# Cache tiles kept with rows innermost, turned through two banks, with the second set of compression weights loaded by halves

## What is computed

```python
def compress_blocks(x, pe, w1, w2):
    B, Tk, H, D = x.shape
    r = CMP_BLOCK // CMP_STRIDE
    c = x.reshape(B, Tk // CMP_STRIDE, CMP_STRIDE, H, D)
    n_cmp = Tk // CMP_STRIDE - r + 1
    blocks = jnp.concatenate([c[:, j:j + n_cmp] for j in range(r)], axis=2)
    blocks = blocks + pe[None, None, :, None, :].astype(x.dtype)
    flat = jnp.moveaxis(blocks, 3, 2).reshape(B, n_cmp, H, CMP_BLOCK * D)
    return jax.nn.silu(flat @ w1) @ w2
...
k_cmp = compress_blocks(kv[:, :, 0], cmp_pe[0], cmp_w1[0], cmp_w2[0])
v_cmp = compress_blocks(kv[:, :, 1], cmp_pe[1], cmp_w1[1], cmp_w2[1])
```

## Time and profile before

| | us |
|---|---|
| median of three runs | 1488.47 (1487.07 to 1491.72) |
| the profiled execution | 1491.82 |
| its span, first to last instruction | 1490.2 |
| PE / DVE / ACT / POOL busy | 1316.0 / 818.9 / 341.5 / 195.6 |
| PE idle before turns, by DVE's copies to `kT` (L1724) | 34.6 |
| products: PE busy at L829, 1024 instructions | 167.6 |
| sums: DVE busy at L1739, 64 instructions | 109.1 |

### The profile page before, as it was taken

One profiled execution on the slowest core, in us unless ns is written; L12 is line 12 of the kernel. 1 busy time (PEld: TensorE's weight loads), 2 busy tenths in 40 slices (PEclk: granted clock), 3 DMA queues, 4 the chain that ended last, 5 costly groups with the idle time before them and its releaser, 6 DMA issues.

```text
span 1490.2 us, 26361 instructions
## 1 busy us (share of the span) xinstructions
PE 1316.0 (88%) x10160; PEld 1060.0 (71%) x10160; DVE 818.9 (55%) x1658; ACT 341.5 (23%) x895; POOL 195.6 (13%) x295
## 2 busy tenths in 40 slices
PE   7996898748884889899999999987788879999996
PEld 3453676537774678789999975675555458999996
DVE  1805546656665666166677429517623405677752
ACT  2114434323320222110000011236734311000000
POOL 0102000101201110111111011060012211111100
PEclk9996799859997999999999999857889989999998
DMA  7438597856636354145444543260036664454340
GB/s 251 155 114 291 193 344 257 290 160 200 196 113 227 115 193 146 33 138 163 131 142 134 195 154 129 63 176 1 1 120 193 197 212 134 149 170 152 118 156 33
DMA packets 148704, 236.14 MB, mean 158 GB/s; under 512 B 10562, under 2 KB 111170, under 8 KB 148162
## 3 DMA queue, kind: packets, MB, share of 16 engines
q1 hardware_dynamic: 140370, 204.00, 41.5%
q0 software_dynamic: 8208, 30.44, 6.2%
HBM read 229.09 MB, written 13.64 MB: 163 GB/s over the span
## 4 chain that ended last, share of the span: by engine, by line
PE 74%; DVE 12%; issue 4%; DMA 3%; SPq 3%; ACT 3%; POOL 0%; POOLq 0%; DVEq 0%; ACTq 0%
PE ps L745 18%; PE ps L540 10%; PE ps L770 10%; PE ps L504 10%; PE ps L829 4%; PE ps L713 4%; DVE big L1739 4%; PE ps L645 2%; PE ps L723 2%; PE ps L843 2%; PE ps L950 2%; PE ps L546 1%; SPq L390 1%; SPq L496 1%; DMA ring<-in_state_win 1%
## 5 line engine op out<-in xcount | busy, mean ns | idle before, releaser
L504 PE MATMUL ps<-ct,ring 128*128 128x128 f32 x960 | 149.9, 296 | 58.3 <-DVE kT L1724 34.6
L504 PEld LDWEIGHTS ps<-ct,ring 128*128 128x128 f32 x960 | 111.7, 149 | 104.0 <-issue 61.7
L829 PE MATMUL ps<-big,proj 128*128 128x168 f32 (+1 forms) x1024 | 167.6, 318 | 17.9 <-DMA proj<-in_cmp_w 15.5
L829 PEld LDWEIGHTS ps<-big,proj 128*128 128x128 f32 x1024 | 155.7, 198 | 24.0 <-DMA proj<-in_cmp_w 15.7
L540 PE MATMUL ps<-ring,xT 128*128 128x512 f32 (+1 forms) x384 | 161.3, 576 | 2.7 <-DMA ring<-in_w_in 2.7
L540 PEld LDWEIGHTS ps<-ring,xT 128*128 128x128 f32 x384 | 70.1, 193 | 81.5 <-issue 78.3
L745 PE MATMUL ps<-kT,proj 128*128 128x144 f32 x960 | 124.2, 286 | 0.0
L745 PEld LDWEIGHTS ps<-kT,proj 128*128 128x128 f32 x960 | 120.3, 190 | 0.0
L1078 ACT ACTIVATE big<-ps 128x512 f32<-128x512 f32 (+3 forms) x172 | 87.1, 532 | 112.4 <-PE ps L504 112.2
L2010 POOL DMA_DIRECT2D ring<-in_cache_kv x64 | 35.2, 550 | 382.1 <-issue 225.9
L1981 POOL TENSOR_TENSOR big<-rows 128x576 f32<-128x576 f32 x22 | 51.0, 2317 | 261.4 <-DVE rows L1638 228.1
(11 more groups left out here) (293 smaller groups left out, 2159.4 us busy)
## 6 DMA issues: line engine op xcount, KB each, us to landing
ring<-in_cache_kv SPq DMA_DIRECT2D x128, 512.0 KB, 5.8
ring<-in_w_gu SPq DMA_DIRECT2D x44, 1024.0 KB, 7.7
ring<-in_w_in SPq DMA_DIRECT2D x11, 2048.0 KB, 8.0
ring<-in_w_down SPq DMA_DIRECT2D x16, 1408.0 KB, 6.6
ring<-in_cache_kv SPq DMA_DIRECT2D x128, 128.0 KB, 3.0
ring<-in_cache_kv POOLq DMA_DIRECT2D x128, 128.0 KB, 3.2
ring<-in_w_out SPq DMA_DIRECT2D x4, 2048.0 KB, 9.1
ring<-in_state_win SPq DMA_DIRECT2D x16, 512.0 KB, 5.5
```

Of the source, the lines that this page charges most:

```text
L504: return nc.tensor.transpose(out, in_, C("ident", 0, rows, rows))
L829: last = mm(cmp_out(u, si, n), w1s(s, o)[:, hf * P:(hf + 1) * P], XS[(4 * kp + si) % XB][:, o, 0:n], start=o == 0, stop=o == 7)
```

## The change

1. `KR` is kept with rows innermost: a copy writes 8 x 32 elements, and the sums read every third element.
2. Turns go by two banks, 6 and 4 in turn, so each waits for the copies of the turn two back. `turn_o` of layer 0 moves from bank 4 to bank 7, with waits against `second` and `turn_weights0`, which use it too.
3. In the first round the turns and sums for tile 1 come one product later. DVE's `combine` moves from the last product of a unit to the first of the next, `silu_cmp` one further product on.
4. The value weights are loaded by halves of their columns: half 0 when 28 products are done, half 1 when 32 are; `sum_w1` goes by halves too, on DVE behind products 28 and 32.
5. Since `plan` follows `steps`, ring entries change places: tile 1 comes behind the fourth value load, not before it, and tile 2's slot is freed by the last turn of tile 1, no longer by a value step.
6. At the start the page table goes behind layer 0's first weights, SP does not wait for it, inputs are turned by column halves, and DVE scales the first half when three copies are done.

```diff
-        KR = [x.rearrange("p (h n o) -> p h n o", h=NKV, o=8)
+        KR = [x.rearrange("p (h o n) -> p h o n", h=NKV, o=8)
...
         for i in range(64):
             kp, a = i // 8, i % 8
-            if kp < 7 and a < 4:
-                steps.append(("turned", kp + 1, 2 * a))
+            ta = a - (kp == 0)
+            if kp < 7 and 0 <= ta < 4:
+                steps.append(("turned", kp + 1, 2 * ta))
...
-            if len(freed_at) >= SLOTS and freed_at[-SLOTS] > at[("product", 29, 1)] and (("w1r", 1), None, 0) not in plan:
-                plan.append((("w1r", 1), None, 0))
+            for hf in range(2):
+                if len(freed_at) >= SLOTS and freed_at[-SLOTS] >= at[("product", 26 + 4 * hf, 1)] and (("w1r", 1, hf), None, 0) not in plan:
+                    plan.append((("w1r", 1, hf), None, 0))
...
-            sp.wait_ge(s_page, 16)
...
                     else:
-                        sp.wait_ge(c_h, 30)
+                        cols = slice(name[2] * P, (name[2] + 1) * P)
+                        sp.wait_ge(c_h, 28 + 4 * name[2])
                     for t in range(2):
...
-                turn(ps[4][0:64, P:2 * P], osm[:, i % 2, :]).then_inc(v_t[l], 1)
+                if l == 0:
+                    pe.wait_ge(c_we, seconds_before[i])
+                turn(ps[7 - 3 * l][0:64, P:2 * P], osm[:, i % 2, :]).then_inc(v_t[l], 1)
...
-                if 8 * kp + g >= 1:
-                    pe.wait_ge(k_a[1], 8 * kp + g)
-                    pe.wait_ge(k_d[1], 8 * kp + g)
+                if 8 * kp + g == 1:
+                    pe.wait_ge(r_ps[0], 6)
+                    pe.wait_ge(r_sg, 6)
+                if 8 * kp + g >= 2:
+                    pe.wait_ge(k_a[1], 8 * kp + g - 1)
+                    pe.wait_ge(k_d[1], 8 * kp + g - 1)
                 for r in range(4):
                     a = (b2 * NPG + half * 4 + r) * KVW + i2 * P
-                    last = turn(ps[6][:, r * P:(r + 1) * P], cmp_src[0][:, a:a + P])
+                    last = turn(ps[6 - 2 * half][:, r * P:(r + 1) * P], cmp_src[0][:, a:a + P])
...
-                    if si == 0 and u >= 1:
+                    if si == 1 and u >= 1:
                         silu_cmp(u - 1)
...
-                x = ps[6][64:128, :].rearrange("p (n o r) -> p n o r", o=8, r=2)
+                x = ps[6 - 2 * half][64:128, :].rearrange("p (n o r) -> p n o r", o=8, r=2)
                 for par in range(2):
-                    last = v.tensor_copy(KR[b2][par * 64:par * 64 + 64, 2 * i2 + 1, 32 * half:32 * half + 32, :], x[:, :, :, par])
+                    last = v.tensor_copy(KR[b2][par * 64:par * 64 + 64, 2 * i2 + 1, :, 32 * half:32 * half + 32],
+                                         x[:, :, :, par].rearrange("p n o -> p o n"))
...
-                    x = [KR[b2][:, :, c:c + 3 * NG - 2:3, :].rearrange("p h m o -> p o h m") for c in range(4)]
+                    x = [KR[b2][:, :, :, c:c + 3 * NG - 2:3] for c in range(4)]
...
-                    if a % 4 == 3:
-                        combine(i // 4)
-                    if i == 31:
-                        sum_w1(1)
-                    if kp < 7 and 3 <= a < 7:
-                        sum_chunks(kp + 1, a - 3)
+                    if i == 63:
+                        combine(15)
+                    elif i and a % 4 == 0:
+                        combine(i // 4 - 1)
+                    if i in (28, 32):
+                        sum_w1(1, i // 32)
+                    sa = a - 3 - (kp == 0)
+                    if kp < 7 and 0 <= sa < 4:
+                        sum_chunks(kp + 1, sa)
```

More of the change, by code:

```diff
@@ L191, in rep @@
             return a.broadcast_to(shape)
-        s_page, s_x, s_first, s_const, s_kv, s_out, s_w1 = (sem(n) for n in ("s_page", "s_x", "s_first", "s_const", "s_kv", "s_out", "s_w1"))
+        s_gain, s_x, s_const, s_kv, s_out, s_w1 = (sem(n) for n in ("s_gain", "s_x", "s_const", "s_kv", "s_out", "s_w1"))
         s_slot = [sem(f"s_slot{i}") for i in range(SLOTS)]
@@ L294, in trunk @@
             steps.append(("product", i, 0))
-            if kp < 7 and a < 4:
-                steps.append(("turned", kp + 1, 2 * a + 1))
+            if kp < 7 and 0 <= ta < 4:
+                steps.append(("turned", kp + 1, 2 * ta + 1))
             steps.append(("product", i, 1))
@@ L304, in trunk @@
         at = {s: n for n, s in enumerate(steps)}
+        seconds_before = [sum(at[("second", k)] < at[("back", i)] for k in range(8)) for i in range(4)]
+        backs_before = [sum(at[("back", i)] < at[("second", k)] for i in range(4)) for k in range(8)]
         freed_at = []
@@ L420, in _ @@
             sp.dma_start(proj[0:TS, 2, 0:D], x_sample.rearrange("b q d -> (b q) d")).then_inc(s_x, 16)
-            sp.dma_start(gc[:], gcol).then_inc(s_first, 16)
-            sp.dma_start(pages[:], page_table.rearrange("b n -> (b n)").unsqueeze(0)).then_inc(s_page, 16)
+            sp.dma_start(gc[:], gcol).then_inc(s_gain, 16)
             def late_constants():
+                sp.dma_start(pages[:], page_table.rearrange("b n -> (b n)").unsqueeze(0)).then_inc(s_const, 16)
                 sp.dma_start(ct[:, n_first:], consts[:, n_first:]).then_inc(s_const, 16)
@@ L438, in _ @@
                     if name[1] == 0:
+                        cols = slice(0, CH)
                         sp.wait_ge(t_p[0], 12)
@@ L504, in turn @@
                 return nc.tensor.transpose(out, in_, C("ident", 0, rows, rows))
-            pe.wait_ge(s_x, 48)
-            pe.wait_ge(s_first, 32)
-            for t in range(3):
-                for j in range(2):
+            pe.wait_ge(s_x, 64)
+            for j in range(2):
+                for t in range(3):
                     for i in range(4):
@@ L777, in second @@
                     pe.wait_ge(c_we, kp)
+                if backs_before[kp]:
+                    pe.wait_ge(v_e[0], backs_before[kp])
                 for b2 in range(2):
@@ L1078, in copy @@
                 return f(out, in_, ACT.Copy)
-            for t in range(3):
-                for j in range(2):
-                    act.wait_ge(x_t, 2 * t + j + 1)
+            for j in range(2):
+                for t in range(3):
+                    act.wait_ge(x_t, 3 * j + t + 1)
                     v = ps[2 * t + j][:, :].rearrange("p (i n) -> p i n", i=4)
@@ L1246, in keep_cmp @@
                     act.wait_ge(c_x, 4 * kp)
-                x = ps[6][0:64, :].rearrange("p (n o r) -> p n o r", o=8, r=2)
+                x = ps[6 - 2 * half][0:64, :].rearrange("p (n o r) -> p n o r", o=8, r=2)
                 for par in range(2):
-                    last = copy(KR[b2][par * 64:par * 64 + 64, 2 * i2, 32 * half:32 * half + 32, :], x[:, :, :, par])
+                    last = copy(KR[b2][par * 64:par * 64 + 64, 2 * i2, :, 32 * half:32 * half + 32],
+                                x[:, :, :, par].rearrange("p n o -> p o n"))
                 last.then_inc(k_a[1], 1)
@@ L1743, in sum_chunks, with sum_w1, part @@
                 last.then_inc(c_x, 1)
-            def sum_w1(k):
-                A, B = proj[:, 0, 0:8 * CH], proj[:, 1, 0:8 * CH]
-                dve.wait_ge(s_w1, 32 * (k + 1))
-                dve.wait_ge(c_h, 32 * k)
-                tt(proj[:, 2, 0:8 * CH], A, B, ALU.add).then_inc(c_b, 1)
-                tt(proj[:, 0, 8 * CH:12 * CH], A[:, 0:4 * CH], B[:, 0:4 * CH], ALU.subtract)
-                tt(proj[:, 1, 8 * CH:12 * CH], A[:, 4 * CH:8 * CH], B[:, 4 * CH:8 * CH], ALU.subtract).then_inc(c_b, 1)
+            def sum_w1(k, hf=0):
+                cols = slice(hf * P, (hf + 1) * P) if k else slice(0, CH)
+                def part(t, c):
+                    return proj[:, t, c * CH:(c + 4) * CH].rearrange("p (i n) -> p i n", n=CH)[:, :, cols]
+                dve.wait_ge(s_w2 if hf else s_w1, 32 if hf else 32 * (k + 1))
+                if k:
+                    dve.wait_ge(c_h, 28 + 4 * hf)
+                tt(part(2, 0), part(0, 0), part(1, 0), ALU.add)
+                tt(part(2, 4), part(0, 4), part(1, 4), ALU.add).then_inc(c_b, 1)
+                tt(part(0, 8), part(0, 0), part(1, 0), ALU.subtract)
+                tt(part(1, 8), part(0, 4), part(1, 4), ALU.subtract).then_inc(c_b, 1)
             def combine(u):
```

33 lines of the change are left out of this document (19 added, 14 removed).

## The result

The changed kernel takes 1449.4 us (median of four runs, 1443.1 to 1453.5) against 1488.2: a ratio of 0.973 (95% interval 0.969 to 0.977). Run again it takes 1446.5 (1444.4 to 1449.1), 0.970 (0.968 to 0.972). The forecast, 1442 with a range of 1429 to 1459, has the direction and holds the time; its middle is 4 to 7 us too low. The profiled execution of after takes 1447.0 (span 1445.1), 44.9 less than that of before, where the sum said 47. The runs from e5_no_delay on were taken on another chip than those from e1_again to e4_old_layout: the kernel before, run beside them, took 1488.9 and 1489.6, and 1491.8 beside the others. So across the two groups ratios and stretches compare better than times.

A forecast was written before the change was run, and what follows sets the result against it. TensorE was taken as the longest chain, with holes mostly from turns waiting for VectorE's copies out of PSUM. Gains 2.0 + 14.5 + 13.4 + 11.5 + 5.8 = 47 us turn 1491.8 into 1445, median 1442, range 1429 to 1459.

The forecast's parts named there:

- start: Kernel start: first weight load no longer waits for the page table, scaling begins after half the copies; 2.0 us gained.
- tile 0's first turn to tile 2's: 298 to 361.94: 8.2 from tile 0's turns, 8.1 and 2.0 from waits, less 3.8 new wait; net 14.5 us gained.
- rounds of tiles 1 to 3: Second-turn waits of 1.8, 4.2 and 4.4 us go, with 1.5 of slow clock behind each of two; 13.4 us gained.
- value weights, to tile 5's fifth turn: Loading by halves cuts tile 4's last turn to tile 5's fifth from 47.5 to 35, less 1 for clock; 11.5 us gained.
- rounds of tiles 5 to 7, to the projection: Copy waits and slow clock behind them go (10.3 us), new value-step waits of 2.0 to 2.5 each; net 5.8 us gained.
- The prologue: Tile 0's eight turns: pitch falls from 2.14 to 1.09 us and the first sum is 0.8 shorter; 8.2 us gained.
- The new wait at tile 2: Before tile 2's first turn: its slot is freed one product later, the load needs 14.4 us, so TensorE waits 3.8.
- The signs named ahead: Signs of being right: copy waits, sums, tile 2's wait of about 4 us, value weights' wait, and clock over 0.92.
- the signs of being wrong: Copies over 1 us each, value steps waiting over 4 us in each round, or half 1 landing after +38.
- Slower copies: Rival: VectorE's PSUM copies slow at 64-byte steps; from about 3 us per turn's pair the kernel is slower; chance 0.04.
- Loads take the waits over: Rival: half 1 late and six round boundaries lose 1.5 more each; 17.5 us of gain goes, 1459; chance 0.17.
- the two neighbouring cases: Rivals on either side of the forecast: more gain, 1430 (chance 0.14), and loads taking the waits over, 1459 (0.17).

The follow-up runs named there:

- e5_no_delay: Changed kernel with item 3 undone (tile 1's turns and sums one product earlier, combine and silu one step earlier): 1439.0 us, ratio 0.966.
- e1_again: The changed kernel itself run once more, unedited, as the mark for the other runs: 1446.5 us, ratio 0.970.
- e4_old_layout: Changed kernel with item 1 undone (old layout of the turned tiles, sums read at a step of 96 bytes): 1449.9 us, ratio 0.971.
- e2_one_bank: Changed kernel with item 2 undone for the turns (all in bank 6, each waiting for the copies of the turn before): 1461.0 us, ratio 0.979.
- e3_whole_weights: Changed kernel with item 4 undone (value weights loaded whole when 30 products are done, summed at product 31): 1451.4 us, ratio 0.971.
- e8_slots: Changed kernel with half 1 summed behind product 35 and ring slots given by which comes free first, not in rotation: 1412.2 us, ratio 0.948.
- e7_sum_late: Changed kernel with one move: VectorE sums half 1 of the value weights behind product 35, not 32: 1437.7 us, ratio 0.965.
- e10_slots_whole: e8_slots with the value weights loaded and summed whole again (item 4 undone, so the later sum goes too): 1426.2 us, ratio 0.957.
- e6_old_start: Changed kernel with item 6 undone (page table first, SP waits for it, inputs turned by row tiles, gains after all six copies): 1448.1 us, ratio 0.971.
- e11_slots_nodelay: e8_slots with item 3 undone (tile 1's turns and sums one product earlier, combine and silu one step earlier): 1409.7 us, ratio 0.945.

## Why the prediction was right, and where not

The sum was made at the output projection: 47 us. There it measures 46.2 (612.83 to 566.67), or 43.2 in e1_again. By its steps, in us gained, the second number of a pair being e1_again:

| step | forecast | measured |
|---|---|---|
| start | 2.0 | 3.5, 0.6 (mean of twelve: 1.7) |
| tile 0's first turn to tile 2's | 14.5 | 17.9, 18.6 |
| rounds of tiles 1 to 3 | 13.4 | 12.6, 12.4 |
| value weights, to tile 5's fifth turn | 11.5 | 10.8, 10.7 |
| rounds of tiles 5 to 7, to the projection | 5.8 | 1.4, 0.9 |

**The start.** The working has TensorE begin at 8.17 in either case; in after it begins at 7.14, where it no longer waits for `gc`, whose load ended the wait in before. The projection starts 2.75 earlier in after and 1.67 in e1_again, about as forecast.

**The prologue** came out larger. The sums cost 1.10 and not 1.3. And the 8.1 us wait had the lower clock behind it, which was not charged: the turn at its end takes 1.09 instead of 0.60, and with the half product and the value step behind it (1.31 and 1.92 elsewhere) some 2.7 us are lost there. In before:

```profile
330.12 2.46 PE L829 MATMUL ps<-big,proj 128*128 128x169 f32 x8
...
332.51 3.01 PE L695 MATMUL ps<-ring,qT 128*32 128x512 f32 x16
```

The new wait at tile 2 was forecast at 3.8 and is 4.31.

**Rounds 1 to 3**: the total is 0.8 short, in part by luck. Where 1.8 was forecast nothing was gained (32.3 us from tile 2's first turn to tile 3's in both kernels), since the lower clock follows the 4.31 us wait: 341.48 has 2.45 us, at a granted 0.50, for eight matmuls that take 1.31. The 1.5 us of slow clock that the forecast put behind each of two waits are in the rows of before: behind the 4.16 the turn takes 1.08 us instead of 0.60 and eight matmuls of half a product take 2.28 instead of 1.31, at a granted 0.50 to 0.54. The other two places gained 5.9 and 6.6, where 5.7 and 5.9 were forecast. That the waits for copies are gone is shown; which item takes them away is not, since they stay away with one bank, with the long sums and with the combine moved back (e2, e4, e5), each undone alone. No run undoes two of them together. Single undoings in all cost 14.5, 4.8, 3.3 and 2, less 6 for the delay, some 19 of the 45 us.

**Value weights**: the chain of landings holds. In us from tile 4's last turn (414.63): the value step at 23.0 (22.6 said), half 1 at 31.5 (29.5), the fifth turn at 36.7 (36); the four weight sums take 2.4 and not 2.6, and the pace of L1562 gives 2.4 too. But it was put down to the halves, and e3_whole_weights shows that they give 6.7 of it; undoing the banks costs 3.5 at the same place (40.3 in e2_one_bank). The working had half 1's issue at 21 and did not ask where the whole load would stand with the new list, which is the same place.

**Rounds 5 to 7** is the term that failed: 5.8 forecast, 1.4 and 0.9 measured. The waits 1.49, 2.27, 2.25 and 3.41 make 9.4 where 7.5 was said, and the lower clock behind half 1 (452.17 to 455, granted 0.50: some 2 us) and in the value step at 513.81 (3.44 instead of 1.92) takes the rest. In the forecast each removed wait brought 1.7 of clock back, and each new one cost 1 or nothing.

**The signs named ahead**: no wait for a copy over 1 us but the one behind half 1 (5.32; the next 0.3), sums between 0.9 and 1.5, about 4 us at tile 2, a wait of TensorE for the value weights under 10 us (none of its own, 5.32 behind VectorE's) and a clock over 0.92 (0.94) all hold. None of the signs of being wrong came: copies take 0.427 us, of three value steps that wait one does so for over 4 us (5.14), and half 1 is there at 31.5.

**Rivals.** Slower copies: with PSUM read at steps of 64 bytes instead of 8, VectorE's take 0.427 us and ScalarE's 0.377, as before. *Loads take the waits over* is half true: most of what is left ends at loads, 26.4 us, but they ate less of the gain than that rival's 17.5. That these loads could start earlier, the prediction did not ask; e8_slots leaves the 6 ahead of tile 0 and 2.0 of the 20.4 in the stretch.

**The range**: its ends are about the times of the two neighbouring cases themselves (1430 and 1459), and not half way to them as the working says; both medians lie inside the forecast's own ends, 1434 to 1452, too.

The 4 to 7 us between forecast and medians are partly the term that failed, partly scatter of the clock and of what lies behind the stretch (873.4 to 880.0, with no edit there). What decides how long the clock stays low in a given run stays open.

## What to carry to other kernels

When waits for one engine are taken out of a loop with rotating buffers, list each load's issue beside the event that frees its buffer: here most of the waits that were left stood there, 20 us in the stretch, and giving a load the buffer that came free first was worth 25 us on top (e7_sum_late to e8_slots). When a part is priced by undoing it, compare runs that differ in that part alone: the halves give some 4 us of stretch beside the early sum and 12 beside the later one, and when e10_slots_whole is held against e3_whole_weights, which differ in the sum and in the slots, that looks like an effect of the slots. And charge each new wait of several us with the lower clock behind it, as each removed one is credited with it: in after, waits of 4.31, 5.32 and 3.41 had it (half products of 2.45 and 2.46 us instead of about 1.3, a value step of 3.44 instead of 1.92), those of 2.25 and 2.27 had not (1.31 and 1.92).

## What was not expected of the hardware

- How long the lower clock lasted behind a wait did not follow the length of the wait. At the value step of tile 7's round it is 13.1 us to the round's last turn behind a wait of 0.94 (e3_whole_weights, clock 1.00 in the step), and 16.3, 14.7, 16.3, 17.6 and 14.6 behind waits of 2.16, 2.46, 2.72, 2.98 and 3.41 (e7_sum_late, e5_no_delay, e1_again, e6_old_start, after): the longest wait has the shortest time but the first. The mean clock in these five steps is 0.71, 0.50, 0.67, 0.50 and 0.53. Whether this is what scatters the runs (10.5 us over eight of the changed kernel, 1.9 over four of e8_slots, but 5.1 over four of e11_slots_nodelay) isn't settled.
- VectorE's sums of 672 elements take 1.71 us at a step of 96 bytes and 1.10 at 12 bytes. The prediction's 0.86, worked out from the 1.26 us that 1056 contiguous elements take, is not reached; why a step of 12 bytes takes 1.10 is not shown.
